# A GLA and MLA encoder step on one core: cached keys loaded turned, a value product one head later, a reordered tail

## The reference, cut to what matters

```python
# layer A
x <- x + rmsnorm((rmsnorm(o) * silu(gate)) @ a_w_out)
# shared keys and values
ckv, krope = rmsnorm(h @ kv_w_down[:, :256]), rope(h @ kv_w_down[:, 256:])
k = concat(ckv_all @ kv_w_uk, krope_all);  v = ckv_all @ kv_w_uv
# layer B, per head
s = einsum('bqhd,bshd->bhqs', q, k) * scale           # block-causal for the prompt
p = softmax(s);  o = einsum('bhqs,bshd->bqhd', p, v)
x <- x + rmsnorm((o * silu(gate)) @ b_w_out)
```

## Time and profile before

| | us |
|---|---|
| median of three runs | 751.51 |
| the profiled execution, its own time | 748.36 |
| its span | 746.6 |
| PE busy | 668.5 |
| DVE busy | 444.0 |
| ACT busy | 294.9 |
| POOL busy | 178.8 |

### The profile page before, as it was taken

How to read it: one execution, slowest core, us unless ns; L and a number is a source line. 1 busy time by engine, 2 the same in 40 slices (tenths; PEclk the granted TensorE clock), 3 DMA queues, 4 the chain that set the end, 5 groups by cost and what they waited for, 6 DMA issues and landing times.

```text
span 746.6 us, 12627 instructions
## 1 busy us (share of the span) xinstructions
PE 668.5 (90%) x4954; PEld 632.7 (85%) x4954; DVE 444.0 (59%) x651; ACT 294.9 (39%) x564; POOL 178.8 (24%) x179
## 2 busy tenths in 40 slices
...
GB/s 305 91 0 58 101 13 104 185 56 112 125 64 169 57 176 142 57 58 137 68 79 88 134 36 6 138 105 100 61 60 60 45 31 58 64 2 278 34 1 141
DMA packets 73261, 67.19 MB, mean 90 GB/s; under 512 B 13154, under 2 KB 69730, under 8 KB 73075
## 3 DMA queue, kind: packets, MB, share of 16 engines
...
...
## 4 chain that ended last, share of the span: by engine, by line
PE 61%; DVE 22%; ACT 8%; issue 5%; POOL 2%; DMA 0%; SPq 0%; DVEq 0%; ACTq 0%; POOLq 0%
PE bank L1265 19%; PE bank L1266 19%; PE bank L1267 19%; DVE slab_lo L979 4%; DVE pT_lo L979 2%; ACT prob L937 1%; DVE oT_lo L979 1%; DVE hat_lo L979 1%; PE bank L1305 1%; DVE sT_lo L979 1%; ACT slab_hi L767 1%; DVE stat L1241 1%; DVE kN_lo L979 1%; DVE stat L1215 1%; PE bank L1457 1%
## 5 line engine op out<-in xcount | busy, mean ns | idle before, releaser
L1265 PE MATMUL bank<-slab_hi,hat_hi 128*128 128x256 f32 (+1 forms) x600 | 173.4, 289 | 15.1 <-DVE hat_lo L979 10.0
L1266 PE MATMUL bank<-slab_lo,hat_hi 128*128 128x256 f32 (+1 forms) x600 | 171.5, 286 | 0.0
L1267 PE MATMUL bank<-slab_hi,hat_lo 128*128 128x256 f32 (+1 forms) x600 | 171.2, 285 | 0.0
L1265 PEld LDWEIGHTS bank<-slab_hi,hat_hi 128*128 128x128 f32 x600 | 118.3, 197 | 17.6 <-DVE hat_lo L979 10.6
L1266 PEld LDWEIGHTS bank<-slab_lo,hat_hi 128*128 128x128 f32 x600 | 118.6, 198 | 0.0
L1267 PEld LDWEIGHTS bank<-slab_hi,hat_lo 128*128 128x128 f32 x600 | 118.4, 197 | 0.0
L979 DVE TENSOR_TENSOR slab_lo<-stage,slab_hi 128x1024 fp32r<-128x1024 f32 (+4 forms) x75 | 91.0, 1213 | 18.5 <-ACT slab_hi L767 16.1
L1265 PE MATMUL bank<-hat_hi,slab_hi 128*128 128x320 f32 (+1 forms) x272 | 86.0, 316 | 1.3 <-DVE slab_lo L979 0.9
L767 ACT ACTIVATE slab_hi<-stage 128x1024 fp32r<-128x1024 f32 (+4 forms) x75 | 74.5, 994 | 28.6 <-issue 14.5
L1266 PE MATMUL bank<-hat_lo,slab_hi 128*128 128x320 f32 (+1 forms) x272 | 85.0, 313 | 0.0
L1267 PE MATMUL bank<-hat_hi,slab_lo 128*128 128x320 f32 (+1 forms) x272 | 84.8, 312 | 0.0
...
## 6 DMA issues: line engine op xcount, KB each, us to landing
...
```

Of the source, the lines that this page charges most:

```text
L1265: pe.matmul(out, a[0], b[0], start=first, stop=False)
L1266: pe.matmul(out, a[0], b[1], start=False, stop=False)
L1267: return pe.matmul(out, a[1], b[0], start=False, stop=last)
```

## The change

Four things are edited.
1. The host passes the cache a second time, turned (`ckvT`, `kropeT`), and the key weights turned (`w_ukT`). `wt` is gone, and `qabs` reads the slab. `ct` and `cr` leave PE and its banks: SP loads `sT_raw` and, twice, `sk_raw`; ACT writes `sT_hi` and `skS` from them, and POOL, no longer DVE, writes `sT_lo` and `skL`. The original rows still come as `craw` for `cs`.
2. `N` is divided: DVE computes the factor, ACT multiplies the probabilities with it.
3. `sv` of turn `h - 1` now follows `T` of turn `h`, `cs` stands after it, and `cx` comes another turn later.
4. The order and the slabs of the latent stage, the tail, and the output projection of layer A change: `y` of layer A waits tile by tile.

```diff
+    def absorbed(h):
+        return ("b_w_uq", 0, KQ, h * (NOPE + ROPE), NOPE, "b_q_norm"), ("w_ukT", h, h + 1, 0, KL, None)
...
-    pre = {("pre", p): [list(nope(2 * p + i)) for i in range(2)] for p in range(HB // 2)}
+    pre = {("pre", p): [list(absorbed(2 * p + i)) for i in range(2)] for p in range(HB // 2)}
...
+SLAB_AT["pre", 1] = SLAB_AT["pre", 2] = SLAB_AT["pre", 0]
+SLAB_AT["gb", 0] = SLAB_AT["gb", 1]
...
+            out += [("oT", t) for t in range(NT - EARLY_GATE, NT)]
             load(("wo", "A", 1))
-            out += [("oT", t) for t in range(NT - EARLY_GATE, NT)]
...
-        out += [("y", ph, 0), ("so",), ("soh",)]
+        out += [("y", ph, 0), ("cx", SB - 1), ("ldk",)]
+        load(("wo", ph, 1))
+        out += [("so",), ("soh",)]
...
-    out += [("gb", 2, 0)] + [("qT", t) for t in range(NT)] + [("gb", 2, 1)]
+    out += [("gb", 2, 0)] + [("qT", t) for t in range(NT)] + [("qr", 0), ("qr", 1), ("gb", 2, 1)]
     load(("gb", 1))
-    out += [("qr", 0), ("qr", 1), ("gb", 1, 0), ("qrT", 0), ("qr", 2), ("qrT", 1), ("qr", 3), ("qrT", 2), ("qr", 4)]
+    out += [("qrT", 0), ("qr", 2), ("qrT", 1), ("qr", 3), ("qrT", 2), ("qr", 4)]
     load(("pre", 0))
...
+    out += [("gb", 1, 0), ("qrT", 3), ("qns", 0), ("qrT", 4), ("qabs", 0)]
     load(("pre", 1))
+    out += [("gb", 1, 1), ("qns", 1)]
     load(("gb", 0))
+    out += [("qabs", 1)]
     load(("pre", 2))
+    out += [("gb", 0, 0), ("qns", 2), ("qabs", 2)]
     load(("pre", 3))
+    out += [("gb", 0, 1), ("ldc", 0), ("ldc", 1)]
     load(("hd", 0))
+    out += [("qns", 3), ("qn", 0), ("kh", 0), ("qabs", 3)]
     load(("hd", 1))
+    out += [("ct", 0), ("cr", 0)]
...
-        out += [("S", h, 0), ("S", h, 1), ("N", h, 0), ("N", h, 1)]
...
+        out += [("S", h, 0), ("S", h, 1), ("N", h, 0), ("N", h, 1), ("ss", h)]
+        if h > 1:
+            out += [("cx", h - 2)]
...
-        out += [("T", h, 0), ("T", h, 1), ("st", h)]
+        out += [("T", h, 0), ("T", h, 1)]
+        if h:
+            out += [("sv", h - 1)]
+        out += [("cs", h), ("st", h)]
...
+    out += [("cx", SB - 2), ("sv", SB - 1)]
     load("uv")
...
-    "S": ("pe", "dve", "act"), "T": ("pe", "act", "dve"), "O": ("pe", "dve"), "ct": ("pe", "act", "dve"),
-    "cr": ("pe", "act", "dve"), "ss": ("pe", "dve", "act"), "cs": ("pool",), 
+    "S": ("pe", "dve", "act"), "T": ("pe", "act", "dve"), "O": ("pe", "dve"), "ct": ("act", "pool"),
+    "cr": ("act", "pool"), "ss": ("pe", "dve", "act"), "cs": ("pool",), 
...
-                        after(sp, "pe", "wt", 2)
+                        after(sp, "pe", "gb", 0, 1)
...
+                    sp.dma_start(sT_raw[b % 2][:, :, :], dram["ckvT"][b]).then_inc(cache_in[b % 2], 16)
+                    for i in range(2):
+                        sp.dma_start(sk_raw[b % 2][i * ROPE:(i + 1) * ROPE, :], dram["kropeT"][b]).then_inc(cache_in[b % 2], 16)
...
+                elif kind == "ct":
+                    after(pool, "act", *step)
+                    b = step[1]
+                    last = pool.tensor_tensor(sT_lo[b % 2][:, :, :], sT_raw[b % 2][:, :, :], raw(sT_hi[:, :, :]), SUB)
...
+                elif kind == "N":
+                    _, h, u = step
+                    for j, (i, c0) in enumerate(zip(UNITS[u], (0, UNITS[u][0] + 1))):
+                        v = prob[u][:, c0:c0 + i + 1, :]
+                        last = act.activation(v, v, ACT.Copy, scale=S1(("S", h, u), stat2, j))
...
+                        after(act, "pe", "ss", b - 1)
...
+                    last = copy(sT_hi[:, :, :], sT_raw[b % 2][:, :, :])
...
+                    if name[0] == "wo" and name[1] == "A":
+                        after(pe, "dve", "oT", t)
...
-                    after(pe, "act", "wt", step[1])
...
-                    after(pe, "dve", "cr", b)
+                    after(pe, "pool", "cr", b)
```

More of the change, by code:

```diff
@@ L243, in latent_layer @@
         out += [("O", h), ("Oh", h)]
[L244 to L250, removed]
+        if h + 2 < HB and h % 2:
+            out += [("vh", h // 2 + 1)]
+    out += [("cx", SB - 2), ("sv", SB - 1)]
     load("uv")
-    out += [("cx", SB - 1), ("ldk",)]
-    load(("wo", "B", 1))
 PARTS = {
@@ L391, in program @@
         post = sb("post", [P, D])
+        lat_gain_at = place[0]
         lat_gain = sb("lat_gain", [P, KL])
@@ L446, in program @@
         thb = sb("thb", [P, TOK])
-        wT = pair("wT", [P, 2 * KL])
         qN_s = pair("qN_s", [P, 2 * P])
@@ L476, in program @@
         kN = pair("kN", [P, SEQ])
-        sT = pair("sT", [P, KC, PAST])
+        sT_hi = sb("sT_hi", [P, KC, PAST], fp32r)
+        sT_lo, sT_raw, skL, sk_raw = [], [], [], []
+        for i in range(2):
+            sT_at = place[0]
+            sT_lo.append(sb(f"sT_lo{i}", [P, KC, PAST], fp32r))
+            place[0] = sT_at
+            sT_raw.append(sb(f"sT_raw{i}", [P, KC, PAST]))
         cn = pair("cn", [P, PAST // P, KL])
@@ L480, in program @@
         skS = sb("skS", [P, PAST], fp32r)
-        skL = sb("skL", [P, PAST], fp32r)
+        skL_at = place[0], gate_at
         sprob = sb("sprob", [P, NT, P])
+        assert place[0] <= phase_at
+        for i, at in enumerate((skL_at[0] + 4 * NT * P, gate_at)):
+            place[0] = at
+            skL.append(sb(f"skL{i}", [P, PAST], fp32r))
+            place[0] = at
+            sk_raw.append(sb(f"sk_raw{i}", [P, PAST]))
+            assert place[0] <= (hat_at if i else phase_at)
+        place[0] = lat_gain_at
         ctxn = sb("ctxn", [P, KL])
-        assert place[0] <= phase_at
         place[0] = hat_at
@@ L499, in program @@
             craw.append(sb(f"craw{i}", [P, PAST // P, KL]))
-        place[0] = gate_at
-        kraw = [sb(f"kraw{i}", [P, PAST // P, ROPE]) for i in range(2)]
         pb = [ctx.enter_context(nc.psum_tensor(f"bank{i}", [P, 2, 512], fp32)) for i in range(NBANK)]
@@ L748, in _ @@
                     last = pool.tensor_tensor(cn[1][:, :, :], craw[b % 2][:, :, :], raw(cn[0][:, :, :]), SUB)
+                elif kind == "ct":
+                    after(pool, "act", *step)
+                    b = step[1]
+                    last = pool.tensor_tensor(sT_lo[b % 2][:, :, :], sT_raw[b % 2][:, :, :], raw(sT_hi[:, :, :]), SUB)
+                elif kind == "cr":
+                    after(pool, "act", *step)
+                    b = step[1]
+                    last = pool.tensor_tensor(skL[b % 2][:, :], sk_raw[b % 2][:, :], raw(skS[:, :]), SUB)
                 elif kind == "rx":
@@ L922, in _ @@
                     last = copy(qN_s[0][:, :], bank[:, 0, 0:2 * P])
-                elif kind == "wt":
-                    copy(wT[0][:, :], bank[:, 0, :])
-                    last = copy(wT[1][:, :], bank[:, 1, :])
                 elif kind == "kh":
@@ L1233, in _ @@
                     last = low(oT_lo[:, h, 0:SEQ], gateT[:, h, 0:SEQ], qS[:, h, :])
-                elif kind == "ct":
-                    last = low(sT[1][:, :, :], bank[:, :, :], sT[0][:, :, :])
-                elif kind == "cr":
-                    low(skL[0:ROPE, :], bank[0:ROPE, 0, :], skS[0:ROPE, :])
-                    last = low(skL[ROPE:P, :], bank[0:ROPE, 0, :], skS[0:ROPE, :])
                 elif kind == "ss":
@@ L1451, in _ @@
                             last = mm3(bank[:, 0, i * P:(i + 1) * P], cut(w, A_, k), cut(qlT, A_, k, slice(SEQ, TOK)), k == 0, k == KQ - 1)
-                elif kind == "wt":
-                    for j, x in enumerate(weights(("pre", step[1]))):
-                        for i in range(2):
-                            for c in range(KC):
-                                at = i * PIECE + KQ * NOPE + c * NOPE
-                                last = pe.transpose(bank[:, j, (i * KC + c) * P:(i * KC + c + 1) * P], raw(x[:, at:at + NOPE]), ident)
                 elif kind == "kh":
```

64 lines of the change are left out of this document (25 added, 39 removed).

## The result

The changed kernel took 772.84 us (median of 4 runs, 769.11 to 774.26) against 750.92 for the kernel before: ratio 1.028, 95% interval 1.024 to 1.033. It is slower by 22 us. The forecast was 749.8, and its range ended at 760. The profiled execution took 769.11 us; its span is 766.9 and its mean clock 0.931 (before: 746.6 and 0.952).

A forecast was written before the change was run, and what follows sets the result against it. PE's work was taken to count nearly in full, the turns bound by a ring through POOL. Terms -5.4 + 2.2 - 11.1 + 3.4 = -10.9, plus 9.2 for clock, gave 746.7 profiled, 749.8 us median; range 737 to 760.

The forecast's parts named there:

- the latent stage: Stretch up to the end of the last gate slab, 77.5 us before: forecast 2.2 us longer, bounds -2 and +5.
- the tail: From y(B,0) on: so waits 3.4 us for cx(7), the rest stays the same; +3.4, bounds +2.5 and +4.
- the clock: Half clock after idle lumps of PE: four drops counted, 2.3 us each in the mean, +9.2 us.
- The projection of layer A: Output projection of layer A: both waits and the slow-clock stretch go, -5.4 us, bounds -4.6 and -7.
- The scaling on ACT: Probability scaling in N, taken as 1.9 us a turn on ACT, forecast to cost nothing.
- The doubled cache loads: Cache loads in layer B's turns, 0.64 MB more a stream, forecast to cost nothing.
- the ring: Layer B's turns: sv, POOL's cs and low parts, then ss back to sv; five turns 103.5 us, bounds 86 and 109.
- The last turn: From sv(5) through the last turn and start of the tail to y(B,0): forecast 21.6 us.
- The stretch to `sv(0)`: From the last gate slab to sv(0), until POOL is released: forecast 42.5 us.
- The third rival: Clock falls in every ring turn from a lump ahead of each ss: +8.5, 760 us; chance 0.17.
- The second rival: POOL is not in the way, PE alone bounds the turns: 86 instead of 103.5, 726 us; chance 0.08.
- The fourth: Port collisions: DVE's slab piece or oT_lo holds POOL up to 1.1 us a turn; +3.8, 755 us; chance 0.10.

The follow-up runs named there:

- e4_projA_only: Kernel before with only layer A's projection edited: slab piece of y(A,1) behind the last oT, y waiting tile by tile; 744.25 us.
- e3_old_tail: Changed kernel with the tail in the order of before: cx(7), kept rows and second output slab ahead of y(B,0); 770.40 us.
- e5_filler: Changed kernel with extra matmuls, results overwritten, on PE where it would idle ahead of ss, vh and so; 757.52 us.
- e1_piece_first: Changed kernel with the head slab's piece moved one place earlier, ahead of cs instead of behind it; 751.03 us.
- e6_last_turn: e1_piece_first with cx(5), sv(6) and cs(7) ahead of ss(7) in the last turn, and the old tail; 745.32 us.
- e9_best: Changed kernel with piece, ct and cr ahead of sv(h-1) and cs(h), last turn reordered ahead of T(7), old tail; 736.45 us.

## Why the prediction was wrong

By stretches the changed kernel's profile differs from that of before by -5.9 us up to the latent stage, +6.3 in it, +9.7 from there to `y(B,0)` and +10.2 in the tail, in all 20.3. The forecast at full clock was -5.4, +2.2, -11.1 and +3.4, and +9.2 for the clock.

**Right.** The projection of layer A: forecast -5.4, measured -6.6 alone in e4_projA_only. The trace of the changed kernel agrees (`gb(2,0)` at 415.31 for 421.18), though one trace shows little here: in e3_old_tail, the same up to there, it stood at 422.49. The scaling on ACT at nothing. The doubled cache loads at nothing: no trace names a wait for the cache. The mechanism of the ring in turns without `vh`, `ss` waiting over 4 us for `skL`. The wait of 3.4 ahead of `so`, measured 3.37.

**The step that failed is the ring of the turns**, "5 of them go round this ring, 2 x 20.3 + 3 x 20.9 = 103.5". It measured 120.5, from 541.82 to 662.34. In turns with `vh` I let only ACT be late, for 0.6. I had not followed what `vh` itself needs: the head slab's piece of the same turn, behind `cs` and the gain. So the ring of these turns is another one, `cs` 3.5, gain 0.9, ACT 0.95, DVE 1.1, `vh` 2.8, `S` 3.6, `ss` 3.0, `qn` 2.2, `kh` 1.4, `T` 1.1, `sv` 1.8: 22.4 us before any handoff, an estimate from the prediction's prices and the DVE row above. With the clock held (e5_filler) these three turns take 22.9 for the 20.9 forecast, and the two others 20.6 for 20.3: 6.4 us in five turns (109.9 for 103.5), nearly all of it this miss. `skL`, priced at 1.2, took 1.6 in the ring. The other 10.6 are half clock, which I had set at four places in all, two of them in the ring; it came in all five turns. From the latent stage on I counted four drops, and the trace of the changed kernel has nine. My bound of 109 for this part left both out. e1_piece_first shows how they hang together: one step moved, and 21.8 us go.

**The last turn** I had at 21.6; it measured 23.0 from POOL's release. The stretch to `sv(0)` had 42.5 and took 44.9. Together the three took 188.4 us for the 167.6 forecast, and so 9.7 more than before where 11.1 less was forecast.

**The tail.** The wait was right and its cause as told, but 12 us at half clock behind it were priced as one drop of 2.3; together +10.2 for +3.4 (and its 2.3). e3_old_tail and e6_last_turn show also that moving `cx(7)` back is not enough: a wait goes with the late `cs(7)`, a consequence of the ring that I had not followed to the end.

**The latent stage** I had at +2.2, measured +6.3 (83.8 for 77.5 us). Its waits are 1.9 ahead of `qr(0)` for 1.8, 3.1 ahead of `qrT(2)` for 2.2, 0.3 and twice 1.15 ahead of `qabs` as forecast, and 0.4 ahead of `gb(0,0)` for 1.85. What was missing is the clock: it fell at 474 and 491 us, and the +2.2 had no drop in it. Its mean of 0.94 is 5.0 of 83.8 us, more than the whole miss of 4.1. In eleven traces with the new order, `gb(2,0)` to `ss(0)` took 97.7 to 102.9 us, 100.3 in the mean, in three with the old one 96.6 to 98.2, 97.2 in the mean. So the new order is 3 us longer there in spite of the turned loads. No run took this stage alone.

**The third rival**, half clock in every ring turn, was the nearest, at 760 and a chance of 0.17. It had the slow matmuls in the ring, and lacked the miss at `vh` and the length of the drop behind `so`. The second rival, PE alone as the bound, needs another order: e9_best comes near it, with 90.6 us for the five turns where I had 86. The fourth, collisions on the port, is there but small: in the turns POOL's `skL` took 1.59 to 1.61 us with DVE's `oT_lo` in its first half microsecond, and 1.26 at 512.75, where it ran without.
